# Gated DeltaNet heads of a decoder layer: doubling levels on 32x32 and 64x64 tiles of the array, and the inverse applied chunk by chunk

## The chip, the core and the metric

The kernel runs on one core of one Trainium2 chip. The metric is the device time of one launch in microseconds; lower is better. TensorE is PE in the profile, VectorE DVE, ScalarE ACT, GpSimd POOL, SyncE SP.

## What is computed

One inference step of a one-layer hybrid decoder: 1024 prompt rows and 8 sample rows of width 1024. A dilated attention branch and a gated DeltaNet branch of 8 heads (DK = DV = 128) are mixed, then comes a feed-forward part. The change lies in the DeltaNet branch. The reference has it in chunks of C = 64 (the kernel takes 128, which gives the same result):

```python
A = jnp.where(strict, jnp.einsum('bhncd,bhnmd->bhncm', kb, k) * decay, 0.0)
T = lax.linalg.triangular_solve(A + eye, jnp.broadcast_to(eye, A.shape), left_side=True,
                                lower=True, unit_diagonal=True)
u = T @ vb
w = T @ (kb * jnp.exp(gc)[..., None])
attn = jnp.einsum('bhncd,bhnmd->bhncm', q, k) * decay
def step(S, xs):
    q_c, k_c, u_c, w_c, attn_c, gc_c = xs
    v_new = u_c - w_c @ S
    o_c = (q_c * jnp.exp(gc_c)[..., None]) @ S + attn_c @ v_new
    ...
```

## The kernel before

The phases follow one another: norm and attention (0 to 449 us of the profiled execution), the heads (to 1283), the mixing, the output projection and the feed-forward part. `heads_block` runs 8 turns. In turn i each engine works on two things at once: `recur_pe`, `recur_act` and `recur_dve` do the recurrence of head i, and a `Filler` feeds in the projection of head i+1 (`project_pe`, `project_act`, `project_dve`) in steps. There are 24 steps a tile (3 column groups x 8 contraction tiles) and 6 tiles (gate A, q, k, v, gate B, z), so 144 steps a turn; each is three fp32r products, L275 to L277, of 352 or 328 columns. Turn 7 has only the two gate tiles, 48 steps, and the last stores. Ahead of turn 0 the projection of head 0 runs by itself.

Where a step goes is written by hand in `per_slot` (L2754); `done` is its running sum, and `fill.slot(p)` on an engine runs the filler up to `done[p - lag]`, with lag 0 on PE and 1 on ACT and DVE. The slots that matter: BASE (4), 44 steps long, DIAG (5), INVERSE (6 to 8, one a level), APPLY (9, 10), SCAN (11 to 18, one a chunk), TAIL (19, 20). On DVE the filler holds at tile m, n = 24 m: the scale (L2958, 0.75 us) and three pairs of convolution taps (L2963 and L2966) of the tile before it, at n, n+4, n+8 and n+12; silu (L2932) at n+20; the low part of a weight tile (`lo`, L271) at n+24.

The inverse of a head's 8 chunks (NT = 8), each 128x128, is made so: diagonal blocks of 16x16 of `ea` (which then holds minus the masked, decayed Gram matrix) go to DRAM and back (`base_to`), VectorE inverts all 64 at once (`invert_base`), and they come back into the transposed inverse `ub` (`base_from`, L3031). PE turns `ub` (L3087), ACT copies it to `t_sb`. Three doubling levels (16 to 32, 32 to 64, 64 to 128) follow, each on full 128x128 tiles in two halves of four chunks: X = A T (L3099), masked by DVE with `level_mask` into `x_sb` (L3336); Y (L3117, or L3119 at the last level), added by DVE (L3344, L3346). From the second level on PE also turns T (L3104) and ACT copies it (L3215) to have both T and its transpose.

Then `APPLY`: u (L3126) and w (L3130) of all chunks, evicted by ACT (L3221) and DVE (L3350). Then the scan: for each chunk PE does m1 = w S (L3141) and the state's part of the output (L3144), one filler step, then waits for DVE's v_new = u - m1 (L3357), and does m3 (L3147, into the new state, L3360) and the rest of the output (L3148), then three filler steps. ACT evicts the output (L3227, L3228). `sm` is the event of the new state, `vn` that of v_new. The wait orders are in program order on every engine. `ea` and the other operands are fp32, so one product is two records in the trace and a transpose one.

Of the kernel before, what the change touches and what calls it, by code (L numbers as in the profile page):

```python
# [14 lines left out]
ACT = mybir.ActivationFunctionType  # L15
# [3 lines left out]
P = 128  # L19
# [61 lines left out]
def build(nc, a, o):  # L81

    ctx = ExitStack()
    with ctx:
# [2597 lines left out]

        hs = ExitStack()
# [4 lines left out]
        def heads_block(used):  # L2688
# [5 lines left out]
            with ExitStack() as place:  # L2694
# [24 lines left out]
            base = u_sb[0][:NB * NT].rearrange("p a b -> p (a b)")[:, :SUB * SUB]  # L2719
            prod = u_sb[1][:NB * NT].rearrange("p a b -> p (a b)")[:, :SUB * SUB // 4]  # L2720
            ub = sb(s, "ub", F8)
# [13 lines left out]
                      xm=2 * LEVELS, xs=2 * LEVELS, ym=2 * LEVELS, tc=2 * LEVELS - 2, ut=2 * LEVELS - 2, uc=2 * LEVELS - 2, uf=2,  # L2735
                      diag_t=2, t0=2, bs=2 * (SUB - 2) + 1, kbe_m=1,
                      kdec_m=1, uw=4, u_ev=2, w_ev=2,
# [16 lines left out]
            per_slot = [10, 2, 3, 3, 44, 4] + LEVELS * [6] + [4, 2] + NT * [4] + [18, 4]  # L2754
# [269 lines left out]
            def base_from(sp, i):  # L3024
# [4 lines left out]
                for b in range(NB):  # L3029
                    r = slice(SUB * b, SUB * b + SUB)  # L3030
                    sp.dma_start(ub[r, :, r], base_scr[1, b].rearrange("c r q -> r c q")).then_inc(base_in, 16)  # L3031

            def recur_pe(pe, i, fill):
# [47 lines left out]
                t_bank, u_bank, x_bank = (7, 4), (3, 5), (6, 5)  # L3081
# [3 lines left out]
                for b in range(2):  # L3085
                    for p in range(4):
                        last = nc.tensor.transpose(banks[t_bank[b]][:, p * P:(p + 1) * P], ub[:, 4 * b + p], ident[:])  # L3087
                    inc(last, "diag_t")
                fill.slot(DIAG)
                for lev in range(LEVELS):  # L3090
                    fill.upto(done[INVERSE + lev] - 6)
                    for b in range(2):
                        n = 2 * lev + b
                        if lev:
                            wt(pe, "tc", i, n - 1)
                        else:
                            wt(pe, "t0", i, b + 1)
# [590 lines left out]
```

## Time and profile before

| | |
|---|---|
| median of 3 runs | 2257.81 us (2252.76 to 2260.27) |
| the profiled execution's own time | 2251.64 us |
| its span, first to last instruction | 2249.9 us |
| granted TensorE clock, mean | 0.981 |
| the heads | 449 to 1283 us, 104.3 us from head to head |

The page gives busy time by engine over the span. A row of a timeline merges records that follow one another: start, length from the first start to the last end, and the count after x. Records of matmuls overlap with those that follow them, so a mean of 275 ns is not what one costs in a long row. The form `64*128 64x128` reads: weights of 64 rows by 128 columns, moving data of 64 rows by 128 columns.

### The profile page before, as it was taken

What the parts mean: (1) busy time and instruction counts of PE and PEld (TensorE: products, weight loads), DVE (VectorE), ACT (ScalarE), POOL (GpSimd) and SP (SyncE); (2) the same over time, 40 slices, a digit from 0 to 9 for tenths busy, and PEclk for the clock granted to TensorE, in tenths of its full rate; (3) what the DMA queues carried; (4) which work ended last, traced back from release to release, by engine and by line L of the source; (5) the groups of instructions that cost most, each with busy time, mean ns of one, the idle gap of its engine ahead of it and who ended that gap; (6) DMA issues with size and microseconds to landing.
All of it is one profiled execution on the core that took longest, in us unless ns stands there. A gap on an engine that the chain in (4) does not pass through costs nothing. (4 is left out here: it accounts for less than half of the span.)

```text
span 2249.9 us, 35996 instructions
## 1 busy us (share of the span) xinstructions
PE 2154.2 (96%) x14198; PEld 2008.8 (89%) x14198; DVE 1328.9 (59%) x2414; ACT 778.5 (35%) x1743; POOL 202.6 (9%) x143
## 2 busy tenths in 40 slices
PE   8999999999999999999998799988999999989998
PEld 6898988799999999999998698768999999977775
DVE  4342314675766666675656434446766667656977
ACT  4332323234242423343333302444333233344343
POOL 0000000011010101010101000000000000007841
PEclk9999998999999999999999899999999999999999
DMA  6102024321221212130322245412322332267474
GB/s 200 47 28 88 17 74 120 76 65 56 60 64 51 81 44 80 35 96 21 94 76 74 93 160 203 143 58 66 87 77 85 89 89 84 70 233 260 153 257 157
DMA packets 233680, 219.98 MB, mean 98 GB/s; under 512 B 35683, under 2 KB 194704, under 8 KB 233522
## 3 DMA queue, kind: packets, MB, share of 16 engines
q1 hardware_dynamic: 191736, 171.98, 25.1%
q10 hardware_dynamic: 38878, 35.84, 4.6%
q0 software_dynamic: 2944, 10.49, 1.7%
q8 instruction: 83, 1.36, 0.2%
q14 instruction: 39, 0.32, 0.0%
HBM read 166.28 MB, written 54.54 MB: 98 GB/s over the span
## 5 line engine op out<-in xcount | busy, mean ns | idle before, releaser
L275 PE MATMUL bank<-xT_hi,w_lo 128*128 128x352 f32 (+1 forms) x1152 | 393.5, 342 | 0.0
L277 PE MATMUL bank<-xT_hi,w_hi 128*128 128x352 f32 (+1 forms) x1152 | 371.2, 322 | 0.0
L276 PE MATMUL bank<-xT_lo,w_hi 128*128 128x352 f32 (+1 forms) x1152 | 370.0, 321 | 0.0
L275 PEld LDWEIGHTS bank<-xT_hi,w_lo 128*128 128x128 f32 x1152 | 219.9, 191 | 1.5 <-issue 0.5
L276 PEld LDWEIGHTS bank<-xT_lo,w_hi 128*128 128x128 f32 x1152 | 221.0, 192 | 0.0
L277 PEld LDWEIGHTS bank<-xT_hi,w_hi 128*128 128x128 f32 x1152 | 218.8, 190 | 0.0
L1334 PE MATMUL bank<-xT_hi,f_lo 128*128 128x258 f32 x704 | 199.5, 283 | 0.2 <-DVE f_c L1461 0.2
L1338 PE MATMUL bank<-xT_hi,f_hi 128*128 128x258 f32 x704 | 198.6, 282 | 0.0
L1336 PE MATMUL bank<-xT_lo,f_hi 128*128 128x258 f32 x704 | 198.3, 282 | 0.0
L1334 PE MATMUL bank<-f_thi,f_lo 128*128 128x258 f32 x528 | 149.2, 283 | 1.0 <-DVE f_tlo L1310 1.0
L1338 PE MATMUL bank<-f_thi,f_hi 128*128 128x258 f32 x528 | 149.3, 283 | 0.0
L1336 PE MATMUL bank<-f_tlo,f_hi 128*128 128x258 f32 x528 | 148.8, 282 | 0.0
L1334 PEld LDWEIGHTS bank<-xT_hi,f_lo 128*128 128x128 f32 x704 | 132.8, 189 | 0.4 <-DVE f_c L1461 0.4
L1338 PEld LDWEIGHTS bank<-xT_hi,f_hi 128*128 128x128 f32 x704 | 133.1, 189 | 0.0
L1336 PEld LDWEIGHTS bank<-xT_lo,f_hi 128*128 128x128 f32 x704 | 132.9, 189 | 0.0
L1334 PEld LDWEIGHTS bank<-f_thi,f_lo 128*128 128x128 f32 x528 | 99.8, 189 | 1.2 <-issue 1.2
L1336 PEld LDWEIGHTS bank<-f_tlo,f_hi 128*128 128x128 f32 x528 | 99.7, 189 | 0.0
L1338 PEld LDWEIGHTS bank<-f_thi,f_hi 128*128 128x128 f32 x528 | 99.6, 189 | 0.0
L275 PE MATMUL bank<-a_kv_hi,xT_lo 128*128 128x512 f32 (+1 forms) x216 | 96.8, 448 | 0.7 <-issue 0.7
L2966 DVE SCALAR_TENSOR_TENSOR qkv<-pre,conv_wt,qkv 128x1024 f32<-128x1024 f32 x72 | 92.0, 1278 | 0.0
L276 PE MATMUL bank<-a_kv_lo,xT_hi 128*128 128x512 f32 (+1 forms) x216 | 87.4, 405 | 0.0
L277 PE MATMUL bank<-a_kv_hi,xT_hi 128*128 128x512 f32 (+1 forms) x216 | 87.0, 403 | 0.0
(465 smaller groups left out, 5059.6 us busy)
## 6 DMA issues: line engine op xcount, KB each, us to landing
w_raw<-in_w_in SPq DMA_DIRECT2D x48, 512.0 KB, 3.9
f_raw<-in_w_ffn_in SPq DMA_DIRECT2D x44, 512.0 KB, 4.8
o_wr<-in_w_ffn_out SPq DMA_DIRECT2D x70, 256.0 KB, 4.6
o_sr<-act_scr SPq DMA_DIRECT2D x24, 704.0 KB, 4.2
act_scr<-f_y ACTq DMA_DIRECT2D x22, 512.0 KB, 3.2
gate_scr<-gate ACTq DMA_DIRECT2D x16, 516.0 KB, 3.0
mix_ta<-gate_scr SPq DMA_DIRECT2D x8, 516.0 KB, 4.9
mix_tb<-gate_scr SPq DMA_DIRECT2D x8, 516.0 KB, 5.8
```

Of the source, the lines that this page charges most:

```text
L275: nc.tensor.matmul(out, stat_lo, mov_hi, start=start, stop=False)
L276: nc.tensor.matmul(out, stat_hi, mov_lo, start=False, stop=False)
L277: return nc.tensor.matmul(out, stat_hi, mov_hi, start=False, stop=stop)
L1334: nc.tensor.matmul(bank, lo[j][:, a, k], x_hi[:, k], start=opens and k == 0, stop=False, skip_group_check=True)
L1336: nc.tensor.matmul(bank, hi[j][:, a, k], x_lo[:, k], start=False, stop=False, skip_group_check=True)
L1338: last = nc.tensor.matmul(bank, hi[j][:, a, k], x_hi[:, k], start=False, stop=k == 3, skip_group_check=True)
L2966: nc.vector.scalar_tensor_tensor(y[:, :L], x_[:, tap:tap + L], cw[:, tap:tap + 1], y[:, :L], ALU.mult, ALU.add).then_inc(conv.sem, 1)
```

## The change

1. The first level works only on the 32x32 blocks of the diagonal. `ub` becomes [128, 8, 32]; each chunk's four blocks are products on four tiles of the array (`QUAD`: 32 rows in, 32 columns out, at the same partitions). The turn of `ub` is now a product with the identity, 32 small ones. X is 32 small products, and Y is computed in both orientations (T and its transpose u), 64 small products, so that nothing is turned later.
2. The second level has 16 products for X (two tiles), 8 for the Y that T needs (one tile) and 16 for the Y of the transpose. The third has 8 for X and 8 for Y on 64x64 tiles. The blocks are put into `t64` and `u_sb` by small copies on ACT and DVE; the zeros of both are written once, ahead of the first head.
3. The u and w products and their evictions go. `kbe` holds a plain copy of k, and col 9 the negated factor. In the scan, m1 = k S; DVE makes `rest` = vb - factor * m1; PE applies the inverse to it (`applied`); DVE copies that out as v_new.
4. `per_slot` goes to 2 and 0 in APPLY, 5 in each SCAN slot and 14 in TAIL, the sum being the same. `base`, `prod` and `vnew` have buffers of their own. The mask of a level is no longer cut to its block of the diagonal.

```diff
+        Q32, Q64 = 32, 64
+        QUAD = [slice(Q32 * n, Q32 * n + Q32) for n in range(4)]
+        HALF = [slice(Q64 * n, Q64 * n + Q64) for n in range(2)]
...
-            t_sb = [sb(s, f"t_sb{b}", [P, 4, P]) for b in range(2)]
-            u_sb = [sb(s, f"u_sb{b}", [P, 4, P]) for b in range(2)]
-            x_sb = [w_t[:, 4 * b:4 * b + 4] for b in range(2)]
+            u_sb = sb(s, "u_sb", F8)
             u_val = sb(s, "u_val", F8)
+            def blocks_of(x, first, size):
+                return x[:, first:first + NT * size // P].rearrange("p a b -> p (a b)").rearrange(
+                    "p (c n) -> p c n", n=size)
+            x32, x64, x128 = blocks_of(w_t, 0, Q32), blocks_of(w_t, 2, Q32), blocks_of(w_t, 4, Q64)
+            t16, t32, u32 = (blocks_of(u_val, 2 * n, Q32) for n in range(3))
+            t64 = sb(s, "t64", [Q64, NT, Q64])
             qe = u_val[:].rearrange("p a b -> p (a b)")
-            vnew = [t_sb[0][:, j] for j in range(2)]
+            rest = [u_val[:, 6 + j] for j in range(2)]
+            vnew_sb = sb(s, "vnew", [P, 2, P])
+            vnew = [vnew_sb[:, j] for j in range(2)]
...
-            ub = sb(s, "ub", F8)
+            ub = sb(s, "ub", [P, NT, Q32])
...
-            per_slot = [10, 2, 3, 3, 44, 4] + LEVELS * [6] + [4, 2] + NT * [4] + [18, 4]
+            per_slot = [10, 2, 3, 3, 44, 4] + LEVELS * [6] + [2, 0] + NT * [5] + [14, 4]
...
                 fill.slot(BASE)
                 wt(pe, "an", i, 2); wt(pe, "pt", i, 2); wt(pe, "eq_m", i, 2); wt(pe, "qe_x", i, 2)
                 pe.wait_ge(base_in, NB * 16 * i + NB * 16)
-                for b in range(2):
-                    for p in range(4):
-                        last = nc.tensor.transpose(banks[t_bank[b]][:, p * P:(p + 1) * P], ub[:, 4 * b + p], ident[:])
-                    inc(last, "diag_t")
+                for c in range(NT):
+                    for q in QUAD:
+                        last = nc.tensor.matmul(bank32(7)[q, c], ub[q, c], ident[q, q], start=True, stop=True)
+                inc(last, "diag_t")
                 fill.slot(DIAG)
-                for lev in range(LEVELS):
...
+                wt(pe, "t0", i, 1)
+                for c in range(NT):
+                    for q in QUAD:
+                        last = nc.tensor.matmul(bank32(6)[q, c], ea[q, c, q], t16[q, c], start=True, stop=True)
+                inc(last, "xm")
+                fill.upto(done[INVERSE] - 2)
+                wt(pe, "xs", i, 1)
+                for c in range(NT):
+                    for q in QUAD:
+                        last = nc.tensor.matmul(bank32(7)[q, c], ub[q, c], x32[q, c], start=True, stop=True)
+                inc(last, "ym")
+                for c in range(NT):
+                    for q in QUAD:
+                        last = nc.tensor.matmul(bank32(4)[q, c], x32[q, c], ub[q, c], start=True, stop=True)
+                inc(last, "ym")
+                fill.slot(INVERSE)
+                wt(pe, "tc", i, 1)
+                for c in range(NT):
+                    for n in range(2):
+                        q, r = QUAD[2 * n], QUAD[2 * n + 1]
+                        last = nc.tensor.matmul(bank32(5)[r, c], ea[q, c, r], t32[q, c], start=True, stop=True)
+                inc(last, "xm")
+                fill.upto(done[INVERSE + 1] - 2)
+                wt(pe, "xs", i, 2); wt(pe, "tc", i, 2)
+                for c in range(NT):
+                    last = nc.tensor.matmul(bank32(3)[QUAD[1], c], u32[QUAD[1], c], x64[QUAD[1], c], start=True, stop=True)
+                inc(last, "ym")
+                for c in range(NT):
+                    for n in range(2):
+                        q, r = QUAD[2 * n], QUAD[2 * n + 1]
+                        last = nc.tensor.matmul(bank32(3, 256)[q, c], x64[r, c], u32[r, c], start=True, stop=True)
+                inc(last, "ym")
+                fill.slot(INVERSE + 1)
+                wt(pe, "t_act", i, 1); wt(pe, "t_dve", i, 1)
+                for c in range(NT):
+                    last = nc.tensor.matmul(bank64(6)[HALF[1], c], ea[HALF[0], c, HALF[1]], t64[:, c], start=True, stop=True)
+                inc(last, "xm")
+                fill.upto(done[INVERSE + 2] - 2)
+                wt(pe, "xs", i, 3); wt(pe, "u_act", i, 1); wt(pe, "u_dve", i, 1)
+                for c in range(NT):
+                    last = nc.tensor.matmul(bank64(4)[HALF[0], c], x128[HALF[1], c], u_sb[HALF[1], c, HALF[1]],
+                                            start=True, stop=True)
+                inc(last, "ym")
                 fill.slot(APPLY)
-                wt(pe, "kbe_m", i, 1)
-                for b in range(2):
-                    wt(pe, "uf", i, b + 1)
-                    for p in range(4):
-                        last = nc.tensor.matmul(banks[6 + b][:, p * P:(p + 1) * P], u_sb[b][:, p],
-                                                vb[:, 4 * b + p], start=True, stop=True)
-                    inc(last, "uw")
-                    for p in range(4):
-                        last = nc.tensor.matmul(banks[3 + b][:, p * P:(p + 1) * P], kbe[:, 4 * b + p],
-                                                u_sb[b][:, p], start=True, stop=True)
-                    inc(last, "uw")
                 fill.slot(APPLY + 1)
 
-                wt(pe, "qew", i, 1); wt(pe, "kdec_m", i, 1)
+                wt(pe, "kbe_m", i, 1); wt(pe, "qew", i, 1); wt(pe, "kdec_m", i, 1)
                 for c in range(NT):
-                    ws, ob, db = banks[5], banks[6 + c % 2], banks[3 + c % 2]
-                    if c < 2:
-                        wt(pe, "u_ev", i, c + 1); wt(pe, "w_ev", i, c + 1)
+                    ws, vn, ob, db = banks[5][:, :P], banks[5][:, P:2 * P], banks[6 + c % 2], banks[3 + c % 2]
+                    if c == 0:
+                        wt(pe, "uf", i, 1)
                     wt(pe, "sm", i, c + 1)
-                    inc(nc.tensor.matmul(ws[:, :P], w_t[:, c], state[c % 2][:], start=True, stop=True), "m1")
+                    inc(nc.tensor.matmul(ws, kbe[:, c], state[c % 2][:], start=True, stop=True), "m1")
                     if c >= 2:
                         wt(pe, "osq", i, c - 1)
                     nc.tensor.matmul(ob[:, :P], q_dec[:, c], state[c % 2][:], start=True, stop=False)
+                    fill.upto(done[SCAN + c] - 4)
+                    wt(pe, "rest", i, c + 1)
+                    inc(nc.tensor.matmul(vn, u_sb[:, c], rest[c % 2], start=True, stop=True), "applied")
                     fill.upto(done[SCAN + c] - 3)
...
                 fill.upto(done[BASE])
-                for b in range(2):
-                    wt(act, "diag_t", i, b + 1)
-                    inc(nc.scalar.activation(t_sb[b][:].rearrange("p a b -> p (a b)"),
-                                             banks[(7, 4)[b]][:], ACT.Copy), "t0")
-                for lev in range(LEVELS):
-                    for b in range(2 if lev else 0):
-                        wt(act, "ut", i, 2 * lev + b - 1)
-                        inc(nc.scalar.activation(u_sb[b][:].rearrange("p a b -> p (a b)"),
-                                                 banks[(7, 4)[b]][:], ACT.Copy), "uc")
-                    fill.slot(INVERSE + lev)
+                bank = banks[7][:, :NT * Q32].rearrange("p (c n) -> p c n", n=Q32)
+                wt(act, "qew", i, 1); wt(act, "diag_t", i, 1)
+                inc(nc.scalar.activation(t16, bank, ACT.Copy), "t0")
+                fill.slot(INVERSE)
+                wt(act, "tc", i, 1)
+                nc.scalar.activation(t64[QUAD[0], :, :Q32], t32[QUAD[0]], ACT.Copy)
+                inc(nc.scalar.activation(t64[QUAD[1], :, Q32:], t32[QUAD[1]], ACT.Copy), "t_act")
+                wt(act, "tc", i, 2)
+                for q in QUAD[::-1]:
+                    last = nc.scalar.activation(u_sb[q, :, q], u32[q], ACT.Copy)
+                inc(last, "u_act")
+                fill.slot(INVERSE + 1)
+                fill.slot(INVERSE + 2)
                 fill.slot(APPLY)
-                for b in range(2):
-                    wt(act, "uw", i, 2 * b + 1)
-                    inc(nc.scalar.activation(u_val[:, 4 * b:4 * b + 4].rearrange("p a b -> p (a b)"),
-                                             banks[6 + b][:], ACT.Copy), "u_ev")
                 for c in range(NT):
...
-                for dst, c, name in ((kbe, 6, "kbe_m"), (kdec, 7, "kdec_m")):
-                    inc(nc.vector.tensor_tensor(dst[:], k_tok[:], col[:, c].unsqueeze(2).to_broadcast(F8),
-                                                ALU.mult), name)
+                nc.vector.tensor_scalar(col[:, 9], col[:, 6], -1.0, None, ALU.mult)
+                inc(nc.vector.tensor_copy(kbe[:], kc[:, :L].rearrange("p (a b) -> p a b", a=8)), "kbe_m")
+                inc(nc.vector.tensor_tensor(kdec[:], k_tok[:], col[:, 7].unsqueeze(2).to_broadcast(F8), ALU.mult), "kdec_m")
...
                 fill.upto(done[BASE])
-                for lev in range(LEVELS):
...
+                def bank32(n, first=0):
+                    return banks[n][:, first:first + NT * Q32].rearrange("p (c n) -> p c n", n=Q32)
+                wt(v, "xm", i, 1)
+                inc(nc.vector.tensor_tensor(x32, bank32(6), level_mask[:, 0, :Q32].unsqueeze(1).to_broadcast([P, NT, Q32]),
+                                            ALU.mult), "xs")
+                fill.slot(INVERSE)
+                wt(v, "ym", i, 1)
+                inc(nc.vector.tensor_tensor(t32, t16, bank32(7), ALU.add), "tc")
+                wt(v, "ym", i, 2)
+                inc(nc.vector.tensor_tensor(u32, ub[:], bank32(4), ALU.add), "tc")
+                wt(v, "xm", i, 2)
+                nc.vector.tensor_copy(x64[QUAD[1]], bank32(5)[QUAD[1]])
+                inc(nc.vector.tensor_copy(x64[QUAD[3]], bank32(5)[QUAD[3]]), "xs")
+                fill.slot(INVERSE + 1)
+                wt(v, "ym", i, 3)
+                inc(nc.vector.tensor_copy(t64[QUAD[1], :, :Q32], bank32(3)[QUAD[1]]), "t_dve")
+                wt(v, "ym", i, 4)
+                nc.vector.tensor_copy(u_sb[QUAD[0], :, QUAD[1]], bank32(3, 256)[QUAD[0]])
+                inc(nc.vector.tensor_copy(u_sb[QUAD[2], :, QUAD[3]], bank32(3, 256)[QUAD[2]]), "u_dve")
+                wt(v, "xm", i, 3)
+                inc(nc.vector.tensor_copy(x128[HALF[1]], banks[6][HALF[1], :].rearrange("p (c n) -> p c n", n=Q64)), "xs")
+                fill.slot(INVERSE + 2)
+                wt(v, "ym", i, 5)
+                inc(nc.vector.tensor_copy(u_sb[HALF[0], :, HALF[1]],
+                                          banks[4][HALF[0], :].rearrange("p (c n) -> p c n", n=Q64)), "uf")
                 fill.slot(APPLY)
-                for b in range(2):
-                    wt(v, "uw", i, 2 * b + 2)
-                    inc(nc.vector.tensor_copy(
-                        w_t[:, 4 * b:4 * b + 4],
-                        banks[3 + b][:].rearrange("p (a b) -> p a b", a=4)), "w_ev")
                 fill.slot(APPLY + 1)
-                wt(v, "u_ev", i, 2)
                 for c in range(NT):
                     wt(v, "m1", i, c + 1)
-                    inc(nc.vector.tensor_tensor(vnew[c % 2], u_val[:, c], banks[5][:, :P], ALU.subtract), "vn")
+                    inc(nc.vector.scalar_tensor_tensor(rest[c % 2], banks[5][:, :P], col[:, 9, c:c + 1], vb[:, c],
+                                                       ALU.mult, ALU.add), "rest")
+                    wt(v, "applied", i, c + 1)
+                    inc(nc.vector.tensor_copy(vnew[c % 2], banks[5][:, P:2 * P]), "vn")
...
+                        nc.vector.memset(t64[:], 0.0)
+                        nc.vector.memset(u_sb[:], 0.0)
                         nc.vector.memset(ub[:], 0.0).then_inc(cleared, 1)
```

## Rows read from the trace of the kernel before

**Rows 1.** The page: span, busy time of each engine.
```profile
span 2249.9 us, 35996 instructions
PE 2154.2 (96%) x14198; PEld 2008.8 (89%) x14198; DVE 1328.9 (59%) x2414; ACT 778.5 (35%) x1743; POOL 202.6 (9%) x143
```

**Rows 2.** Table of windows: one filled head, and the last head.
```profile
core 0: us, PE busy (x) PEld busy (x) DVE busy (x) ACT busy (x) POOL busy (x), PEclk, DMA share, GB/s
553.00:657.00 104.00, 104.00 (x757) 103.62 (x756) 68.33 (x152) 37.55 (x97) 7.82 (x9) 1.00 0.22 61
1179.00:1283.00 104.00, 80.59 (x546) 74.73 (x545) 64.08 (x149) 39.28 (x93) 7.77 (x9) 0.92 0.30 94
```

**Rows 3.** Waits of PE, 440 to 1300 us: total us, times, longest.
```profile
PE bank L3147 <- DVE t_sb L3357: 3.4, 8, 0.6
PE bank L3048 <- DVE ub L3531: 1.5, 1, 1.5
```

**Rows 4.** Groups by line and form, PE: count | busy us, mean ns.
```profile
L3099 PE MATMUL bank<-t_sb,ea 128*128 128x128 f32 x384 | 50.4, 278 | 2.6 <-DVE t_sb L3344 2.4 <-ACT t_sb L3210 0.2
...
L3104 PE MATMUL bank<-ident,t_sb 128*128 128x128 f32 x128 | 19.2, 273 | 0.0
...
L3126 PE MATMUL bank<-vb,u_sb 128*128 128x128 f32 x128 | 17.0, 276 | 1.7 <-DVE u_sb L3346 1.7
...
L3119 PE MATMUL bank<-u_sb,w_t 128*128 128x128 f32 x128 | 15.7, 275 | 0.0
...
L3087 PE MATMUL bank<-ident,ub 128*128 128x128 f32 x64 | 8.3, 273 | 0.0
```

**Rows 5.** Timeline of PE: start us, us, line, records; three stretches.
```profile
97.92 0.31 PE L277 MATMUL bank<-xT_hi,a_q_hi 128*128 128x328 f32 x1
98.17 0.71 PE L314 MATMUL bank<-ident,ba_ch 32*128 32x32 f32 x9
98.80 0.43 PE L275 MATMUL bank<-xT_hi,a_q_lo 128*128 128x352 f32 x1
99.07 0.32 PE L276 MATMUL bank<-xT_lo,a_q_hi 128*128 128x352 f32 x1
...
111.07 0.71 PE L771 MATMUL bank<-a_kT,a_qT 64*128 64x128 f32 x8
...
489.59 1.95 PE L3099 MATMUL bank<-t_sb,ea 128*128 128x128 f32 x16
```

**Rows 6.** Two lines' own loads (ns min/median/max), and one group by form.
```profile
L2478 PEld LDWEIGHTS bank<-sa_onehot,sa_trep x6: 103/107/108, 380.3 to 380.8; 33*32 33x32 f32 x6
...
L3099 PEld LDWEIGHTS bank<-t_sb,ea x384: 186/192/194, 489.4 to 1233.0; 128*128 128x128 f32 x192
...
L2518 PE MATMUL bank<-sa_own,sa_pd 8*32 8x256 f32 x6 | 1.5, 378 | 0.0
```

**Rows 7.** Timeline of PE, then of DVE, in the scan of a filled head.
```profile
624.18 0.38 PE L3141 MATMUL bank<-state,w_t 128*128 128x128 f32 x2
...
625.08 0.38 PE L3147 MATMUL bank<-t_sb,kdec 128*128 128x128 f32 x2
...
616.33 0.23 DVE L2963 SCALAR_TENSOR_TENSOR qkv<-conv_state,conv_wt,qkv 128x8 f32<-128x8 f32 x1
616.47 1.28 DVE L2966 SCALAR_TENSOR_TENSOR qkv<-pre,conv_wt,qkv 128x1024 f32<-128x1024 f32 x1
...
624.60 0.29 DVE L3357 TENSOR_TENSOR t_sb<-u_val,bank 128x128 f32<-128x128 f32 x1 [1.46 <-PE bank L3141]
625.50 0.35 DVE L3360 SCALAR_TENSOR_TENSOR state<-state,eglast,bank 128x128 f32<-128x128 f32 x1 [0.61 <-PE bank L3147]
625.76 1.22 DVE L2932 SCALAR_TENSOR_TENSOR qkv<-tanh,qkv 128x1032 f32<-128x1032 f32 x1
...
628.55 1.22 DVE L271 TENSOR_TENSOR w_lo<-w_raw,w_hi 128x1024 fp32r<-128x1024 f32 x1
629.69 0.75 DVE L2958 TENSOR_SCALAR qkv<-pre,conv_wt 128x1032 f32<-128x1032 f32 x1
```

**Rows 8.** Groups by line and form, DVE: count | busy us, mean ns.
```profile
L3336 DVE TENSOR_TENSOR w_t<-bank,level_mask 128x512 f32<-128x512 f32 x48 | 33.2, 691 | 38.8 <-PE bank L3099 38.8
```

**Rows 9.** Timeline of all engines in the last head.
```profile
1218.58 1.09 PE L3087 MATMUL bank<-ident,ub 128*128 128x128 f32 x8
...
1241.02 0.39 PE L3141 MATMUL bank<-state,w_t 128*128 128x128 f32 x2
...
1245.35 0.49 PE L3141 MATMUL bank<-state,w_t 128*128 128x128 f32 x2 [0.22 <-DVE state L3360]
...
1245.87 0.29 DVE L3357 TENSOR_TENSOR t_sb<-u_val,bank 128x128 f32<-128x128 f32 x1 [0.58 <-PE bank L3141]
```

More of the change, by code:

```diff
@@ L3089, in recur_pe @@
                 fill.slot(DIAG)
-                for lev in range(LEVELS):
-                    fill.upto(done[INVERSE + lev] - 6)
-                    for b in range(2):
[L3093 to L3097, printed above, removed]
-                        for p in range(4):
-                            last = nc.tensor.matmul(banks[x_bank[b]][:, p * P:(p + 1) * P], ea[:, 4 * b + p],
-                                                    t_sb[b][:, p], start=True, stop=True)
-                        inc(last, "xm")
-                        if lev:
-                            for p in range(4):
-                                last = nc.tensor.transpose(banks[t_bank[b]][:, p * P:(p + 1) * P], t_sb[b][:, p],
-                                                           ident[:])
-                            inc(last, "ut")
-                    fill.upto(done[INVERSE + lev] - 2)
-                    for b in range(2):
-                        n = 2 * lev + b
-                        wt(pe, "xs", i, n + 1)
-                        if lev:
-                            wt(pe, "uc", i, n - 1)
-                        for p in range(4):
-                            cs = slice(p * P, (p + 1) * P)
-                            u = u_sb[b][:, p] if lev else ub[:, 4 * b + p]
-                            if lev < LEVELS - 1:
-                                last = nc.tensor.matmul(banks[t_bank[b]][:, cs], u, x_sb[b][:, p], start=True, stop=True)
-                            else:
-                                last = nc.tensor.matmul(banks[u_bank[b]][:, cs], x_sb[b][:, p], u, start=True, stop=True)
-                        inc(last, "ym")
@@ L3332, in recur_dve @@
                 fill.upto(done[BASE])
-                for lev in range(LEVELS):
-                    for b in range(2):
-                        wt(v, "xm", i, 2 * lev + b + 1)
-                        inc(nc.vector.tensor_tensor(
-                            x_sb[b], banks[(6, 5)[b]][:].rearrange("p (a b) -> p a b", a=4),
-                            level_mask[:, lev].unsqueeze(1).to_broadcast([P, 4, P]), ALU.mult), "xs")
-                    fill.slot(INVERSE + lev)
-                    four = lambda bank: banks[bank][:].rearrange("p (a b) -> p a b", a=4)
-                    for b in range(2):
-                        wt(v, "ym", i, 2 * lev + b + 1)
-                        if lev < LEVELS - 1:
-                            inc(nc.vector.tensor_tensor(t_sb[b][:], t_sb[b][:], four((7, 4)[b]), ALU.add), "tc")
-                        else:
-                            inc(nc.vector.tensor_tensor(u_sb[b][:], u_sb[b][:], four((3, 5)[b]), ALU.add), "uf")
@@ L3347, in recur_dve, with bank32 @@
-                fill.slot(APPLY)
-                for b in range(2):
-                    wt(v, "uw", i, 2 * b + 2)
-                    inc(nc.vector.tensor_copy(
-                        w_t[:, 4 * b:4 * b + 4],
-                        banks[3 + b][:].rearrange("p (a b) -> p a b", a=4)), "w_ev")
+                def bank32(n, first=0):
+                    return banks[n][:, first:first + NT * Q32].rearrange("p (c n) -> p c n", n=Q32)
+                wt(v, "xm", i, 1)
+                inc(nc.vector.tensor_tensor(x32, bank32(6), level_mask[:, 0, :Q32].unsqueeze(1).to_broadcast([P, NT, Q32]),
+                                            ALU.mult), "xs")
```

22 lines of the change are left out of this document (10 added, 12 removed).

## The prediction

> **What bounds the kernel now.** The page comes first: TensorE is busy for 96% of the span, VectorE for 59%, ScalarE for 35% [rows 1]. An average says nothing about one stage, so the heads (449 to 1283 us) are read by head in the table of windows. In seven of the eight periods of 104 us TensorE is busy for all 104 at full granted clock, while VectorE is busy for 68 [rows 2]: six columns of numbers, and only PE's equals the length. The eighth, with little projection left to fill in, shows 81 of 104. The waits agree: from 440 to 1300 us PE waited 3.4 us in eight pieces for L3357, all in that last head, and 1.5 us for the clearing of `ub` ahead of the first [rows 3]. So in seven heads a microsecond taken from PE's queue is a microsecond of the end, as long as no new wait appears; the last head is a chain of latencies.
>
> **What leaves PE.** One fp32 product is two records in the trace. Sixteen records of 128 columns in the filled head take 1.95 us, of which the last is 0.275, so they start every (1.95-0.275)/15 = 0.112 us [rows 5]; transposes are one record, 19.2/128 = 0.15 us with their tails, 0.11 at their pace [rows 4]. (The busy time per record in rows 4 counts tails that overlap with the projection; pace is what PE's queue pays.) Per head leave: 48 records of X (L3099), 48 of the three Y products (L3119 stands for three such rows), 32 of u and w (L3126 stands for two), and 16+8 transposes (L3104, L3087) [rows 4]. That is 128 x 0.112 + 24 x 0.11 = 14.3 + 2.6 = 17.0 us.
>
> **What comes.** (a) T applied in the scan: 8 products of 128x128, 16 x 0.112 = 1.8 us. (b) 128 products on 32x32 tiles of the diagonal: turn 32, X 32, Y 64. (c) Level 2: 16 on two tiles in turn, 8 on one, 16 on two. (d) Level 3: 16 products of 64x64 on one tile, 32 records. (e) Seven groups that change the tiling.
> The trace has no 32x32 tile in a long row, so (b) is bounded. What a record costs follows its columns: 0.112 us at 128, and (1.5-0.378)/5 = 0.22 us at 256 on a 32-column tile [rows 6]. Scaled, 32 columns are 0.028. The weights too: a load of 128 columns lasts 192 ns, of 32 columns 107 [rows 6], 0.89 ns a column, 28 ns for 32. With the 5 ns that stand over 128 columns I take 0.032 per record. Do tiles run side by side? L771, whose products alternate between two row halves, has 8 records in 0.71 us [rows 5]: (0.71-0.27)/8 = 0.055 apiece, half of 0.112. Two tiles, half the price. Four tiles: a quarter, 2 x 0.032/4 = 0.016 us a product. Ends: 0.016 (full overlap); 0.032 (only pairs); 0.064 (none). L314 is the row with the smallest tiles, 9 single records in 0.71 us, (0.71-0.22)/8 = 0.062 each [rows 5]; its weights are 128 columns wide, which can explain that, or it is a floor for any record, and a product would be 0.124. I take 0.016, since L771 is the only row with alternating tiles, and keep 0.124 as the far end. Nothing excludes somewhat less than 0.016, but that is at most 2 us a head. So (b) 128 x 0.016 = 2.05; (c) 16 x 0.032 + 8 x 0.064 + 16 x 0.032 = 1.5; (d) 32 x (0.112/2 + 0.002) = 1.9.
> (e) Around L314: L277 starts at 97.92 and streams 0.15, yet L314 starts at 98.17, 0.10 later; its last record starts about 98.68 and the projection resumes at 98.80, and then L276 comes 0.27 behind L275, not 0.16 [rows 5]. 0.10 + 0.09 + 0.11 = 0.3 us a group, 7 x 0.3 = 2.1.
> Sum added: 1.8 + 2.05 + 1.5 + 1.9 + 2.1 = 9.3. PE saves 7.7 us a filled head.
>
> The Trainium skill, TensorE: Matmul & The Clock Gate (Part 3), says that tiles in different row groups run concurrently, some 4 ns apart, and 16 of them gained 10.6 times at 512 columns; L771's halving agrees in kind, and no run here shows four tiles.
>
> **What it starts: VectorE in the scan.** Today a chunk is m1, one step of projection, vn, m3. From L3141 at 624.18 to VectorE's start is 0.42, its subtraction 0.29, and L3147 follows at 625.08, of which 0.45 is four records and 0.45 the step [rows 7]: 0.14 us to spare. The change puts a second such hop in: applied (0.22), one step (0.45), vn. Ready takes 0.42 + 0.29 + 0.06 = 0.77 against 0.67, a wait of some 0.07 to 0.1 per chunk, 0.6 a head. `rest` itself has the cover of m1, q_dec and a step, 0.90 against 0.42 + 0.35 + 0.05, if VectorE is free. It often isn't: its filler comes behind `sm`, and the new `per_slot` bunches it. At chunk 2 its slot now ends at step 96 and holds silu, lo and the first tap: 1.22 + 1.22 + 0.75, back to back 2.95 us [rows 7]; today the slots part it into 1.22 and 1.97. From m3: 0.9 to `sm`, 2.95, `rest` 0.4 = 4.25, against PE's 0.45 + 3 steps 1.4 + 0.45 + 0.45 = 2.8. PE waits 1.4. Ahead of chunk 0 two taps of 1.45 (L2966 and its small partner) are queued between `uf` and `rest`, which today lie beside the u and w products; from Y's end: 0.3 + 0.69 + 2.9 + 0.4 = 4.3 against 4 + 1 steps and m1, 2.8: another 1.4. Together 3.4 us a head. Queued behind the waiting product are the projection's own steps, so nothing covers it.
> With one answer: VectorE loses 14 evictions of 0.69 [rows 8] and gains 10 of a quarter to a half of the size and 8 copies in the scan, and isn't the bound; ScalarE's seven small copies lie beside two to six projection steps; base_to and base_from issue the same number of DMAs, landing in the 44-step slot, and neither they nor the loads behind them move. Clearing u_sb and t64 adds some 0.7 us once, ahead of the first head, where PE already waits for that clearing [rows 3].
> **The last head.** From the turn at 1218.58 to the scan at 1241.02 are 22.4 us [rows 9]. Shorter groups (about 1 us for 1.9), quarter- and half-width evictions and no u/w stage make it 14, saving 8.4. Each chunk gains a hop: L3141 to VectorE 0.52 [rows 9], + 0.29 + 0.05 + 0.07 = 0.93, eight times 7.4. Net 1 us.
>
> **Sum.** 7 x (7.7 - 3.4) = 30.1, + 1 - 0.7 = 30.4 us. The profiled execution took 2251.6 (span 2249.9) and becomes 2221.2; the median of the runs is 6.2 higher, 2257.8, and becomes 2227.4. Say 2227.
>
> **The rivals.**
> Pairs only (0.032 a product): 2.05 us more a head, gain 30.4 - 14.3 = 16, 2242. For: L771 shows two, not four.
> Nothing waits (VectorE drains its bunches in time, cheap changes of tiling): 7 x 7.7 = 54, 2204. Against: VectorE's ledger above.
> The waits take it: if every chunk's `rest` comes 1 us late, 8 + 0.6 us a head stand against 7.7, 7 x 0.9 = 6 lost, 2264. Against: most slots hold one tap of 1.45, which fits.
> No overlap among tiles that write one bank (slower): L771's two write different banks, the new ones all the same. 168 x 0.064 = 10.8 replaces 3.55; added 16.6, so 17.0 - 16.6 - 3.4 = -3.0 a head, -21: 2278. It decides from 0.016 + 4.3/128 = 0.05 us a product upward. The Trainium skill, TensorEngine Tiling (Gotcha 1, PSUM Pressure), says that different row tiles can't access the same PSUM bank simultaneously; by that rule 2278 is the outcome, and no row here tells.
> A floor per record (slower): 168 x 0.124 = 20.8; added 26.8, -9.8 - 3.4 = -13.2 a head, -92: 2349. For: L314's 62 ns. Against: L771's 55, which is two records of a stream that starts them in pairs. The Trainium skill, TensorE: Matmul & The Clock Gate (Part 1), names about 62 ns per matmul where the hardware decoder is off and a floor of some 25 ns where it is on; by the first of these the outcome is this one.
> That it doesn't do what it says could be only in the count: 368 small records in place of 136 wide ones go through PE's queue, which the floor prices.
>
> **How the numbers follow.** Forecast 0.38, pairs 0.20, nothing waits 0.10, waits take it 0.10, no overlap 0.15, floor 0.07. Two runs of this kernel can't be told apart within 0.3% (6.8 us). Faster is the first three, 0.68; same is most of the fourth, 0.08; slower 0.24. The range must reach from between the forecast and 2204 to beyond 2278: 2206 to 2282 leaves out the floor and half of "nothing waits". The likeliest case alone: 2215 to 2240.
>
> **What would show it.** PE's windows by head: period near 100 us, busy a few us short of it. In the timeline, a group of 32 diagonal products in about 0.5 to 0.8 us (0.016), 1.0 (pairs), 2.0 (none), 4 (floor). Gaps of 0.1 and 0.2 us around each group. Waits of PE for `rest` at chunks 0 and 3, 1.4 us each, and under 0.1 for vn elsewhere. I am wrong if the groups take 1.5 us and more, or if PE waits in every chunk.

## The result, and the profile after

The changed kernel takes 2238.05 us (median of 7 runs, 2233.4 to 2242.88), beside 2254.36 us for the kernel before in the same session (7 runs). The ratio is 0.9931, 95% interval 0.991 to 0.9953: 16.3 us, 0.7%, faster, where 30 were forecast. The profiled execution took 2236.37 us. The first rows are the page's, and answer to [rows 1]:

```profile
span 2234.6 us, 39719 instructions
PE 2121.4 (95%) x16054; PEld 1944.5 (87%) x16054; DVE 1312.5 (59%) x2456; ACT 766.2 (34%) x1735; POOL 203.0 (9%) x143
```

The table of windows: one filled head of the kernel after, from its turn (L3104) to the next one's, then its last head in three stages (turn to first product of the scan; scan; to the next phase). Below it the same three stages of the kernel before.

```profile
core 0: us, PE busy (x) PEld busy (x) DVE busy (x) ACT busy (x) POOL busy (x), PEclk, DMA share, GB/s
588.60:689.60 101.00, 98.88 (x995) 94.63 (x995) 66.62 (x157) 35.88 (x96) 7.75 (x9) 1.00 0.23 64
...
1197.50:1213.40 15.90, 10.81 (x369) 9.78 (x368) 8.92 (x16) 5.71 (x10) 0.00 (x0) 0.50 0.22 61
1213.40:1243.10 29.70, 25.73 (x81) 18.98 (x82) 12.82 (x29) 7.68 (x25) 0.00 (x0) 0.50 0.04 14
1243.10:1256.70 13.60, 7.84 (x38) 7.37 (x37) 7.17 (x23) 4.60 (x12) 0.93 (x1) 0.63 0.15 43
```
```profile
1218.60:1241.00 22.40, 18.13 (x153) 17.36 (x152) 13.88 (x19) 7.58 (x12) 0.00 (x0) 1.00 0.21 65
1241.00:1257.10 16.10, 11.07 (x66) 8.24 (x65) 9.50 (x20) 7.59 (x25) 0.00 (x0) 1.00 0.00 1
1257.10:1269.00 11.90, 5.89 (x39) 5.60 (x38) 7.39 (x23) 4.59 (x12) 0.93 (x1) 0.75 0.17 50
```

Two things stand there. A filled head still has a granted clock of 1.00, but it is 101 us long, not 104, and PE isn't busy for all of it (98.9; before, 104 of 104 [rows 2]). And the last head is worse: 15.9 + 29.7 + 13.6 = 59.1 us against 50.4. Its clock is at 0.50 (1.2 GHz) for 45 us on end, where the kernel before had 1.00 (2.4 GHz). The fall itself isn't new: PE waits ahead of both turns, 3.8 us before and 3.9 after, and in the kernel before the clock fell there too and was back by the turn at 1218.6. The wait and the two windows around that turn, of the kernel before:

```profile
PE bank L2830 <- DVE gate L2988: 3.8, 1, 3.8
```
```profile
1215.00:1218.50 3.50, 2.43 (x12) 1.64 (x13) 1.88 (x3) 0.00 (x0) 0.00 (x0) 0.54 0.85 279
1218.50:1222.00 3.50, 3.25 (x27) 2.93 (x26) 0.69 (x1) 2.03 (x3) 0.00 (x0) 0.97 0.21 82
```

From first starts in the trace, the seven periods take 710.1 us (731.7 before), 21.6 less; the last head 8.7 more; the rest of the program 2.4 less; together 15.3 us, the difference of the two profiled executions (2251.64 and 2236.37).

The waits of PE, 440 to 1300 us, against the 3.4 and 1.5 us of [rows 3] (columns: us in total, times, longest):

```profile
PE bank L3168 <- DVE u_val L3386: 13.6, 18, 1.1
...
PE bank L3171 <- DVE vnew L3389: 3.1, 8, 0.4
PE bank L3060 <- DVE ub L3565: 2.3, 1, 2.3
```

L3168 is the applied product, L3386 is `rest`: in the filled heads it waits twice a head, at chunks 0 and 3 (14 of the 18; the other four and all of L3171's are in the last head). What VectorE does ahead of those two chunks, in its timeline:

```profile
606.70 1.27 DVE L2977 SCALAR_TENSOR_TENSOR qkv<-pre,conv_wt,qkv 128x1024 f32<-128x1024 f32 x1
...
608.14 1.28 DVE L2977 SCALAR_TENSOR_TENSOR qkv<-pre,conv_wt,qkv 128x1024 f32<-128x1024 f32 x1
609.34 0.35 DVE L3386 SCALAR_TENSOR_TENSOR u_val<-bank,col,vb 128x128 f32<-128x128 f32 x1
...
618.62 1.23 DVE L2943 SCALAR_TENSOR_TENSOR qkv<-tanh,qkv 128x1032 f32<-128x1032 f32 x1
619.76 1.22 DVE L271 TENSOR_TENSOR w_lo<-w_raw,w_hi 128x1024 fp32r<-128x1024 f32 x1
620.90 0.75 DVE L2969 TENSOR_SCALAR qkv<-pre,conv_wt 128x1032 f32<-128x1032 f32 x1
621.57 0.34 DVE L3386 SCALAR_TENSOR_TENSOR u_val<-bank,col,vb 128x128 f32<-128x128 f32 x1
```

`rest` stands without a gap behind two taps, then behind silu, lo and scaling: VectorE isn't slow, it is late. The tiles themselves, in PE's timeline at a turn:

```profile
588.34 0.32 PE L277 MATMUL bank<-xT_hi,w_hi 128*128 128x352 f32 x1
588.59 0.75 PE L3104 MATMUL bank<-ident,ub 32*32 32x32 f32 x64
589.28 0.43 PE L275 MATMUL bank<-xT_hi,w_lo 128*128 128x352 f32 x1
```

The last record starts 0.12 us ahead of the projection's. So all 64 records of the 32 products start within (589.28 - 588.59 - 0.12 =) 0.57 us, some 9 ns a record and 0.018 us a product: the price of four tiles side by side, tested below.

### The profile page after: what moved, and what is told of

It is laid out like the page before. It is cut to its first block and busy times, and to the rows that moved or that the text cites. A ratio compares the mean times of both kernels' runs of the same rounds, so it can differ in the third digit from the quotient of the medians.

```text
span 2234.6 us, 39719 instructions
## 1 busy us (share of the span) xinstructions
PE 2121.4 (95%) x16054; PEld 1944.5 (87%) x16054; DVE 1312.5 (59%) x2456; ACT 766.2 (34%) x1735; POOL 203.0 (9%) x143
## 5 line engine op out<-in xcount | busy, mean ns | idle before, releaser
L1338 PEld LDWEIGHTS bank<-f_thi,f_hi 128*128 128x128 f32 x528 | 99.5, 189 | 0.0
```

What stands on the lines that cost most here:

```text
L1338: last = nc.tensor.matmul(bank, hi[j][:, a, k], x_hi[:, k], start=False, stop=k == 3, skip_group_check=True)
```

## The experiments

Each was run in five rounds beside the kernel before, whose median was 2252.77 us in the session of the two parts alone and of the unused products in the whole change, 2250.64 in that of the last two below, and 2253.72 in that of the other four. Periods and stages are first starts in the profiled execution. The order is that of the argument.

**One part alone: the tiles.** Inverse as in after; u and w of all chunks ahead of the scan, scan, weights of the decay and `per_slot` as in before.

```diff
-            per_slot = [10, 2, 3, 3, 44, 4] + LEVELS * [6] + [2, 0] + NT * [5] + [14, 4]
+            per_slot = [10, 2, 3, 3, 44, 4] + LEVELS * [6] + [4, 2] + NT * [4] + [18, 4]
+                for b in range(2):
+                    for p in range(4):
+                        last = nc.tensor.matmul(banks[6 + b][:, p * P:(p + 1) * P], u_sb[:, 4 * b + p],
+                                                vb[:, 4 * b + p], start=True, stop=True)
...
```

> One part of the change alone: the inverse on 32x32 and 64x64 tiles as in after, then u and w of all eight chunks ahead of the scan, and scan, filler steps and weights of the decay as in before. By the ledger of one filled head the full-tile inverse costs 12.8 us of TensorE and the tiles 6.4, less 2 us for the changes of tiling: 4.4 us a head over seven heads, 31 us. Theory C (what is missing in the filled heads is the chunk-wise part: 3.5 us removed, 2.1 added, 1.8 us of waits for rest): this kernel is FASTER than the full change in the filled heads, period 99.8 to 100.2 us against 101.2, and 2222 to 2230 us in all, ratio to before 0.986 to 0.989. Rival D (the tiles fall short themselves, through their changes of tiling and thin groups): period 101 or more, 2236 us or more. In the last head the clock may stay at 0.50 here too until the dense products of u and w; then the last head gives back some 3 to 5 us.

Measured: 2211.58 us, ratio 0.9827 (0.9799 to 0.9855). The seven periods take 696.4 us, 99.5 each, so the tiles alone save 35.3 us there, 5.0 a head, and 2.2 us in the last head. Theory C holds, by 10 us more than its range, and D falls: half of the change is worth two and a half times the whole.

**The other part alone: the apply within the scan.**

```diff
-                        last = nc.tensor.matmul(banks[6 + b][:, p * P:(p + 1) * P], u_sb[b][:, p],
-                                                vb[:, 4 * b + p], start=True, stop=True)
...
+                    wt(pe, "rest", i, c + 1)
+                    inc(nc.tensor.matmul(vn, u_sb[c // 4][:, c % 4], rest[c % 2], start=True, stop=True), "applied")
```

> The other part alone: the inverse on full tiles as in before, the apply within the scan chunk by chunk as in after, with after's filler steps. Theory C: per filled head 3.5 us removed, 1.4 + 0.7 us added, 1.8 us of waits for rest: within 0.5 us of before in each, and in the last head the apply stage of some 5 us goes and 0.9 us x 8 of hops come, more if the clock falls in the scan (then up to 8 us more). So 2250 to 2264 us, ratio to before 0.998 to 1.004. Rival D (the chunk-wise part is what brings the gain and the tiles little): 2240 us or less.

Measured: 2281.01 us, ratio 1.0132 (1.0105 to 1.016), 28 us slower than before. Periods 746.4 us, 2.1 a head more than before; the last head 62.9 us, 12.5 more. The direction is theory C's; the size isn't: 11 us was its upper end, and it had each filled head within 0.5 us. Both waits are in the waits of PE (L3137 is the applied product; 440 to 1180 us), and the scan of the last head is at 1.2 GHz though this inverse is of full tiles, so no small tile is needed for that (its windows, inverse and scan):

```profile
PE bank L3137 <- DVE u_val L3340: 14.3, 14, 1.1
```
```profile
1240.10:1259.80 19.70, 14.72 (x123) 13.95 (x121) 12.33 (x18) 6.30 (x9) 0.00 (x0) 0.99 0.21 63
1259.80:1289.40 29.60, 25.16 (x81) 18.49 (x82) 12.74 (x29) 7.67 (x25) 0.00 (x0) 0.52 0.04 16
```

The two halves add up: -5.0 and +2.1 a head against -3.1 for both.

**VectorE's bunches taken apart.** The full change; only the places of VectorE's projection work, and the wait for the inverse, move:

```diff
+                fill.upto(80)
-                fill.slot(APPLY)
-                fill.slot(APPLY + 1)
-                    fill.slot(SCAN + c)
+                    fill.upto((84, 92, 96, 97, 100, 104, 108, 116)[c])
```

> The full change, computing what it computes, with VectorE's projection work spread over the scan: one long step behind each chunk's state instead of two taps ahead of rest of chunk 0 and silu, weight split and scaling (3.1 us together) ahead of rest of chunk 3; the wait for the inverse moves from the chunk's first product to the applied one. Theory E (the two waits for rest, 2.0 us a head, come from VectorE's bunched work, not from the hop itself): they fall to under 0.3 us a head, the period of the filled heads goes from 101.2 to 99.0 to 99.5 us, and the kernel takes 2222 to 2228 us, ratio to before 0.986 to 0.989. Rival F (the chunk-wise scan has one hop too many for its filler, and waits move to another chunk or to vn): period 100.5 us or more and 2234 us or more.

Measured: 2218.09 us, ratio 0.9844 (0.9817 to 0.9872). The waits for `rest` are gone from the filled heads, and the period is 98.9 us, against 101.4 of after (each the mean of seven). Theory E holds, by 4 us more than its range: with the two waits of 1.8 us a head go 0.1 us of longer product starts and the wait of 0.3 us that after has at L3145. No operation of the change was undone for this, so the extra hop by itself makes no wait for `rest`.

**Two steps behind each hop.** As above, and:

```diff
-            per_slot = [10, 2, 3, 3, 44, 4] + LEVELS * [6] + [2, 0] + NT * [5] + [14, 4]
+            per_slot = [10, 2, 3, 3, 44, 4] + LEVELS * [6] + [0, 0] + NT * [6] + [8, 4]
-                    fill.upto(done[SCAN + c] - 3)
+                    fill.upto(done[SCAN + c] - 2)
...
```

The steps of the tail between its own products are fewer accordingly, and VectorE's places move with the steps.

> As e5_unbunch, and two filler steps instead of one between the chunk's first products and the applied one and between that and m3 (six steps a chunk instead of five, the tail gives up six). Theory G (the small loss at m3, 0.07 us of waiting and 0.09 us longer records a chunk, 1.3 us a head, is the vn hop of 0.87 us behind one step of 0.48 us): it goes too, period 97.7 to 98.3 us, 2213 to 2220 us, ratio 0.982 to 0.985, so that the chunk-wise part brings a gain in the filled heads beside the tiles alone (99.2 us). Rival F: the tail, with 8 steps instead of 14, now waits for its own hops, and the period is no lower than that of e5_unbunch.

Measured: 2206.67 us, ratio 0.9794 (0.9768 to 0.982), period 97.4 us. Theory G holds, by 6 us more than its range. It shows in m3's mean duration. In the kernel after, m3's own weights' load starts at 614.22 us, together with its first record; here the load starts at 613.41 and the record at 613.56, so 0.15 us of the load lie behind the record before it. Groups of PE by form, 440 to 1180 us (count | busy us, mean ns), first the kernel after, then this one:

```profile
L3171 PE MATMUL bank<-vnew,kdec 128*128 128x128 f32 x112 | 27.3, 326 | 0.0
```
```profile
L3171 PE MATMUL bank<-vnew,kdec 128*128 128x128 f32 x112 | 21.5, 273 | 0.0
```

No wait is listed in either row: one of 0.07 us ahead of each m3 was too short for the column, and it and the longer record came to 1.3 us a head. With both repairs the chunk-wise part has the sign it was meant to have in a filled head: 97.4 us, against 99.5 with the tiles alone. Some 0.3 of these 2.1 us aren't its own: the tiles alone still have the wait at their third level (7 times, 1.9 us in all) that the moved filler takes away here. The tiles alone with that filler moved weren't run.

**The last head by the old way.** The full change in heads 0 to 6, and `if i == HB - 1:` u and w of all chunks ahead of the scan.

> The full change in heads 0 to 6; the last head alone computes u and w of all chunks ahead of its scan, on the tiles' inverse, as e3_tiles does. Theory H (the last head's 59.1 us against 50.4 of before come from the hop in a scan with no filler, and from the clock that the thin scan leaves at 0.50): turn to first scan product 15.9 to 20 us, scan 29.6 to 16 us at a clock of 1.00, the last head about 48 us, the kernel 10 to 12 us faster than after: 2226 to 2229 us, ratio to before 0.988 to 0.990. Rival: what is late at the end of the last head is not the scan, and the gain is under 4 us.

Measured: 2229.56 us, ratio 0.9894 (0.987 to 0.9918), 8 us below after, whose interval it just overlaps; the last head takes 51.1 us in its trace, 8.0 less than after's, where 48 was expected. The windows of its u and w products, of the scan in the middle and of its last 5 us:

```profile
1217.00:1221.60 4.60, 4.60 (x30) 4.60 (x29) 0.73 (x2) 1.19 (x2) 0.00 (x0) 0.66 0.03 13
...
1226.00:1230.00 4.00, 2.79 (x18) 2.02 (x17) 2.25 (x6) 2.05 (x8) 0.00 (x0) 1.00 0.01 2
...
1234.00:1239.00 5.00, 4.72 (x18) 3.89 (x18) 2.34 (x6) 2.06 (x7) 0.00 (x0) 0.50 0.00 0
```

The clock is back after the dense products of u and w and gone again at the end of the scan; in the tiles-alone kernel it stayed at 1.00 through the same scan, and what makes the difference is open. Theory H holds in its place, at three quarters of its size.

**Clock or hop: dense work in the last head's gaps.** First, four products of 128x128 by 512 in the idle 3.9 us ahead of the turn:

```diff
+                                    for _ in range(4):
+                                        nc.tensor.matmul(banks[7][:], ident[:], k_tok[:, :4].rearrange("p a b -> p (a b)"),
+                                                         start=True, stop=True)
                                 pe.wait_ge(conv_copied, g + 1)
```

> The kernel after, with four products of 128x128 by 512 columns (results unused, into bank 7) in the last head's turn, put where TensorE idles for 3.9 us (1191.0 to 1194.9) before its second group of conv transposes. Nothing else changes. Theory A (the last head loses its time because the granted clock fell to 0.50 in that gap and the small tiles and the thin scan do not bring it back): the clock is 1.00 at the turn of the diagonal blocks. If it then stays up, inverse plus scan of the last head take about 35 us (15.9 + 29.6 = 45.5 now; 22.4 - 8 + 16.1 + 7.4 = 38 by the prediction's sum), and the kernel is 7 to 11 us faster than after, ratio to before about 0.989. If it falls again within the inverse (TensorE busy 2.4 of 3.5 us at 1.2 GHz, so about 1.2 of 3.5 at 2.4 GHz), the gain is 0 to 4 us. Rival B (the last head's loss is the extra hop of the scan, whatever the clock): no change against after, ratio about 0.993.

Measured: 2233.11 us, ratio 0.9918 (0.9893 to 0.9943), not to be told from after's 0.9931. The table of windows shows the clock at the turn up, as theory A has it, and falling some 6 us later, in the midst of the small groups (1199.10 is the turn; the last row is the scan):

```profile
1199.00:1203.00 4.00, 2.39 (x203) 2.00 (x205) 1.85 (x4) 1.33 (x2) 0.00 (x0) 1.00 0.20 79
1203.00:1206.00 3.00, 1.38 (x106) 1.16 (x97) 2.54 (x5) 1.11 (x3) 0.00 (x0) 0.92 0.16 34
1206.00:1210.00 4.00, 3.47 (x64) 3.38 (x64) 1.71 (x5) 3.27 (x6) 0.00 (x0) 0.50 0.50 147
```
```profile
1213.90:1243.50 29.60, 25.67 (x80) 18.89 (x81) 12.71 (x29) 7.68 (x25) 0.00 (x0) 0.50 0.03 13
```

So keeping the clock up through the gap isn't enough: it falls again within the inverse. Second, the same with unused 128x128 products also ahead of the waits of the last head's inverse and scan (and a few waits of their own for what they read and overwrite):

```diff
+                        for _ in range(n):
+                            nc.tensor.matmul(banks[bank][:, :P], ident[:], kdec[:, 0], start=True, stop=True)
...
```

> As e1_gap, and in the last head also small dense work while TensorE waits: 3 or 4 products of 128x128 (0.22 us each at 2.4 GHz, results unused) ahead of each wait of the inverse, and 2, 1 and 2 of them ahead of each chunk's waits for the state, for rest and for vn. Theory A: the granted clock is 1.00 from the turn to the end of the last head's scan, the scan falls from 29.6 to 20 to 23 us and the inverse from 15.9 to 12 to 14, the kernel is 8 to 12 us faster than after: 2226 to 2230 us, ratio to before 0.987 to 0.989. Rival B (the hop, not the clock): the dummy products only lengthen the chain, the kernel is 0 to 5 us slower than after.

Measured: 2232.03 us, ratio 0.9908 (0.9881 to 0.9936), not to be told from after either, where theory A had 8 to 12 us less. Windows: two of the inverse and one of the scan, then the whole scan.

```profile
1214.00:1218.00 4.00, 4.00 (x27) 3.66 (x27) 1.92 (x2) 0.00 (x0) 0.00 (x0) 0.50 0.00 0
1218.00:1222.00 4.00, 4.00 (x27) 3.88 (x26) 1.81 (x2) 0.00 (x0) 0.00 (x0) 0.50 0.39 131
...
1226.00:1230.00 4.00, 3.54 (x27) 3.03 (x26) 2.26 (x6) 1.12 (x4) 0.00 (x0) 1.00 0.00 0
```
```profile
1221.40:1246.00 24.60, 22.75 (x160) 20.53 (x158) 11.88 (x29) 7.67 (x25) 0.00 (x0) 0.92 0.01 2
```

The scan falls from 29.6 to 24.6 us once the clock is back, and the rest up to the next phase from 13.6 to 11.8: rival B, the hop alone, falls. But the inverse rises from 15.9 to 19.1 us, since the unused products ran there in part at 1.2 GHz themselves (eight records take 2.07 us, 1.16 at the higher clock), and little is left. Theory A is right that the clock is part of the cause, in the windows of one profiled execution each, and wrong about the remedy. The scan's 24.6 against 16.1 us of before, with the clock nearly up in both, is the hop: 8.5 us, dummies included.

**Dense products in the gap, tiles alone.**

> e3_tiles with the four unused products of e1_gap in the last head's idle time. By e1_gap the clock is 1.00 at the turn and falls within the inverse. Theory A: turn to first scan product 20.2 to 19 us, 0 to 2 us faster than e3_tiles, ratio to before 0.982 to 0.983. If the dense products at the end of the inverse come before the clock falls, up to 5 us faster, 0.980.

Measured: 2209.17 us, ratio 0.981 (0.9783 to 0.9838), against 0.9827 (0.9799 to 0.9855) without them: a difference that isn't shown. Turn to scan took 21.4 us, not 19 to 20.2, and not less than the 20.3 without them: in windows of 4 us the granted clock is 0.50 from 4 us behind the turn on here; without the dense products it is 1.00 from 4 to 8 us behind it, then 0.56 and 0.50.

**Are the four tiles really side by side?** The full change with the two loops of the turn, X0, Y0a and Y0b exchanged:

```diff
-                for c in range(NT):
-                    for q in QUAD:
+                for q in QUAD:
+                    for c in range(NT):
```

> The full change with only the order of the diagonal groups' products turned round: the turn, X0, Y0a and Y0b (64 records each) issue all eight products of one 32x32 tile of the array, then those of the next, instead of one product on each of the four tiles in turn. Theory O (the 31.5 ns of four records is four tiles working side by side, so each tile needs some 31 ns a record): a tile's 16 records take 16 x 31 = 0.5 us, one group 2.0 instead of 0.5 to 0.7 us, four groups 5.2 to 6 us a head more as far as they are not behind other waits, period 106 to 107.5 us and 2276 to 2290 us, ratio to before 1.010 to 1.016. Rival P (a record of this size costs 8 ns wherever it goes): the same as after, 2238 us. Between: the engine looks ahead over the queue and overlaps some of them.

Measured: 2278.3 us, ratio 1.0126 (1.0103 to 1.015), period 106.2 us in the mean (105.5 in the first five, 108 in the last two, where the granted clock is 0.50 for 7 and 3 us). The turn in PE's timeline:

```profile
591.35 1.91 PE L3104 MATMUL bank<-ident,ub 32*32 32x32 f32 x64
```

The same 64 records take 1.9 us instead of 0.75; from first start to last it is 1.72 us, 27 ns a record, against 9. Theory O holds: the 9 ns of after come from four tiles at work in turn. A group now costs 1.8 us, no less than a full-tile group of the kernel before (1.7). This order comes near to the prediction's rival "no overlap", at 0.054 us a product for its 0.064. That the time is within 1 us of the rival's 2278 is luck: only the diagonal groups are in this order, and beside its own session's 2250.64 the kernel is 28 us slower, where the rival had 21.

**All repairs together.** Both repairs of the scan in heads 0 to 6, u and w ahead in the last head.

> e6_unbunch_split in heads 0 to 6 and the last head of e8_last. If the two repairs add up (period 97.4 us as in e6_unbunch_split; last head 51.1 us as in e8_last against 58.3): 6 to 8 us faster than e6_unbunch_split, 2198 to 2201 us, ratio to before 0.975 to 0.977. If the last head's gain is used up elsewhere at its end: within 3 us of e6_unbunch_split.

Measured: 2200.53 us, ratio 0.9777 (0.9753 to 0.9802), 50 us below before. Its periods take 681.8 us, as without the old way in the last head, which takes 54.1 us here instead of 58.3. That is 4.2 us of the 7.2 expected: its scan has one hop a chunk again, but is at 1.2 GHz from some 6 us in. By the medians it is 6 us below the version with both repairs alone (2206.67), by the ratios 4, and the two intervals overlap.

## Why the prediction was half right

**What leaves and what comes: right within 0.7 us a term.** The groups that left cost PE 16.3 us a head by their starts, not 17.0. The tiles cost 6.4 (from each group's first start to the projection's next), of which 2.6 are the diagonal groups (2.05 forecast), 1.65 level 2 (1.5), 2.1 level 3 (1.9). Full overlap, the choice on which the sign hung, is what happened, and the rivals "pairs only", "no overlap" and "floor" didn't occur: a record every 9 ns is under both figures for a record that the prediction gives beside its floor. The time alone wouldn't have told: 2238 is nearer to the 2242 of "pairs only" than to the forecast. The Trainium skill, TensorEngine Tiling (Gotcha 1, PSUM Pressure), says that different row tiles can't access one PSUM bank simultaneously. The rows here differ from it: four tiles that differ in rows and in columns at once write one bank, and their records start 9 ns apart; no run here shows row tiles of the same columns.

**The changes of tiling: too dear.** 0.3 us a group was read off L314 [rows 5]. After, the last projection record ahead of a small group lasts 0.25 us to the next start instead of 0.16, and the group's last record 0.12 instead of 0.03: 0.09 + 0.09, 1.3 us a head in place of 2.1. (The half behind each group is in the 6.4 as well; it counts once.) With the wait of 0.3 us at the third level, which the prediction had not priced, the tiles' ledger is 12.9 of the 16.3 leaving, 6.4 + 0.65 + 0.3 coming: some 5.5 a head by these starts, 5.0 measured.

**VectorE in the scan: right place, under-priced.** The two waits came where the ledger of VectorE's filler put them, at chunks 0 and 3, 1.8 us together against 2.8, and moving that filler removes them. What was too low are the small ones: "0.07 to 0.1 per chunk" is the wait only. A product that waits at all also starts with its weights' load exposed: m3's two records take 0.33 us to the next start instead of 0.24, so vn cost 1.3 us a head, not 0.6, and `rest` 0.1 more per wait. The chunk-wise part so costs 2.1 us a head where the forecast's own terms (3.6 off, 1.8 and 3.4 on) make 1.6; the tiles bring 5.0 where they make 5.9. Seven times 1.2 us, 8.5 us, is the first half of what is missing.

**The last head: the step that failed.** "Net 1 us" gained was 8.7 lost, the second half. By stages it is 6.5 less in the inverse, 13.6 more in the scan and 1.7 more behind it. The hop was priced well (7.4; some 8.5 measured), the inverse was to take 14 and took 15.9 (14.8 where the clock was up at the turn). What the sum lacked is the clock: it was 1.00 in this stage of the kernel before, and the sum kept it there without a reason, though the change thins out this work and [rows 2] has 0.92 for the head. The fall in the gap ahead of the turn, with its wait of 3.8 us, was in the trace and isn't in the prediction's account of the waits. At 1.2 GHz the scan takes 5 us and the end of the head 1.8 us more, by the windows with the unused products and without. Which property of the work holds the clock down isn't settled: dense products that keep PE busy for 8 us of 8 did not bring it back at once.

**The sum.** With 21.6 - 8.7 + 2.4 = 15.3 the profiled execution is accounted for. The 2.4 us outside the heads aren't explained: 0.6 more ahead of the first turn, where the wait for the clearing is 2.3 us for 1.5 (0.7 more was forecast), and 3.0 less behind the last head. The twelve profiled executions, alike in both stretches but for that clearing, take 485.4 to 493.7 us to the first turn and 974.0 to 980.9 behind the last head, so it may be nothing.

## What to carry to other kernels

A change that couples two parts should be priced, and run, part by part: here one half brought 41 us and the other took 28, and the whole hid both. Where a stage gains a hop between engines, look at what the other engine has queued at that very place, and give each hop more work of cover than its latency: moving existing work, with no operation added or removed, was worth 31 us. On the diagonal, small tiles paid only where consecutive products went to different tiles. And in a stage without filler, price the granted clock too: here it cost the last head some 5 us of scan and 2 behind it, as much as the smaller inverse saved there (6.5).

## What was not expected of the hardware

- In two stretches in a row TensorE shows busy for 4.00 of 4.00 us at a granted clock of 0.50, with 27 records each, and at 1.00 a few microseconds later with 3.54 busy. Busy time in the profile doesn't tell whether the clock stays up.
- A wait of 0.07 us, too short to be listed, doubles its price: the product behind it took 0.09 us longer.
- The order of two loops alone changed a group of 64 records from 0.57 to 1.72 us, first start to last.
- Four unused dense products ahead of the tiles-alone inverse kept the clock up at its turn (0.96), and the inverse was no faster: 21.4 us against 20.3.
